# A sparse mixer on one core: keys in the partitions, softmax and gate as rows of the score product, row maxima and sums among the projections

## The reference, cut to what matters

```python
proj = x @ w_in                                   # q (16 heads x 64), 3 x (k, v) of 4 groups, 48 gates
q = q * HEAD_DIM ** -0.5
gates = sigmoid(gates)                            # one for each branch, head and query
k_cmp = gelu((blocks(k0) + pos0) @ w1_0 + b1_0) @ w2_0      # 31 blocks of 32 tokens, and v_cmp alike
s = q . k_cmp - slope * (t - center);  p_cmp = softmax(mask(s)) * m_c;  o_cmp = p_cmp @ v_cmp
s = q . k1 - slope * dist;  p = softmax(mask(s, dist >= 0));            o_sel = p @ v1
s = q . k2 - slope * dist;  p = softmax(mask(s, 0 <= dist < 512));      o_win = p @ v2
o = gates[0] * o_cmp + gates[1] * o_sel + gates[2] * o_win
return o @ w_out
```

## Time and profile before

| | |
|---|---|
| median of 3 runs | 3488.45 us (3485.4 to 3493.25) |
| profiled execution | 3480.47 us, span of its trace 3478.6 us |
| PE busy | 3188.6 us (92%) |
| VectorE busy | 1927.1 us (55%) |
| ScalarE busy | 1353.0 us (39%) |
| mean granted clock of PE | 0.951 |

### The profile page before, as it was taken

The page is one execution under the profiler, slowest core; times in us unless marked ns, Lnnn a source line. Parts: engine busy times, 40 slices in busy tenths (PEclk is TensorE's granted clock), DMA queues, the critical chain, the costliest instruction groups (busy, mean ns, idle before and its releaser), DMA issues.

```text
span 3478.6 us, 37759 instructions
## 1 busy us (share of the span) xinstructions
PE 3188.6 (92%) x15192; PEld 2546.7 (73%) x15192; DVE 1927.1 (55%) x2960; ACT 1353.0 (39%) x1980; POOL 192.1 (6%) x167
## 2 busy tenths in 40 slices
PE   6988899999999888899889888999999989899998
PEld 3876777777788666677667666888767879778876
DVE  5886666454433667754434774555245469455522
ACT  4244444334432344433443473333224336333321
POOL 0011122210000011100000000000000000000000
PEclk8999999999999899999989999999999879999999
DMA  6221123320012222232003122333322200123331
GB/s 213 71 67 55 57 66 94 99 89 26 23 37 73 73 69 77 58 93 81 25 25 91 55 77 80 97 91 97 92 76 97 79 1 1 49 88 94 91 97 61
DMA packets 77214, 250.93 MB, mean 72 GB/s; under 512 B 8689, under 2 KB 10609, under 8 KB 77041
## 3 DMA queue, kind: packets, MB, share of 16 engines
q1 hardware_dynamic: 71568, 228.60, 21.7%
q0 software_dynamic: 4608, 16.78, 1.6%
q10 hardware_dynamic: 864, 3.15, 0.2%
HBM read 246.39 MB, written 2.10 MB: 71 GB/s over the span
## 4 chain that ended last, share of the span: by engine, by line
PE 41%; DVE 7%; ACT 4%; issue 1%; DMA 0%; DVEq 0%; ACTq 0%; SPq 0%
PE PS L977 30%; PE PS L1410 2%; PE PS L2410 1%; PE PS L1533 1%; PE PS L996 1%; PE PS L2386 1%; ACT WH L938 1%; PE PS L2397 1%; DVE U L2194 1%; PE PS L2387 1%; DVE WL L948 1%; DVE U L1051 1%; PE PS L2333 0%; PE PS L2371 0%; DVE STAT L2664 0%
## 5 line engine op out<-in xcount | busy, mean ns | idle before, releaser
L948 DVE TENSOR_TENSOR WL<-RAW,WH 128x1024 fp32r<-128x1024 f32 (+3 forms) x415 | 485.7, 1171 | 587.4 <-ACT WH L938 586.4
L938 ACT ACTIVATE WH<-RAW 128x1024 fp32r<-128x1024 f32 (+4 forms) x447 | 429.2, 965 | 496.9 <-PE PS L977 399.3
L1410 PE MATMUL PS<-Hh,WH 128*128 128x512 f32 x1376 | 532.4, 387 | 16.7 <-DVE WL L948 8.1
L1410 PE MATMUL PS<-Hl,WH 128*128 128x512 f32 x1376 | 494.9, 360 | 0.0
L1410 PE MATMUL PS<-Hh,WL 128*128 128x512 f32 x1376 | 493.6, 359 | 0.0
L1410 PEld LDWEIGHTS PS<-Hh,WH 128*128 128x128 f32 x1376 | 266.8, 194 | 82.5 <-issue 25.0
L977 PE MATMUL PS<-FHh,WH 128*128 128x512 f32 x768 | 306.1, 399 | 15.1 <-DVE FHl L1042 14.9
L977 PE MATMUL PS<-FHl,WH 128*128 128x512 f32 x768 | 304.8, 397 | 0.0
L977 PE MATMUL PS<-FHh,WL 128*128 128x512 f32 x768 | 304.7, 397 | 0.0
L1410 PEld LDWEIGHTS PS<-Hl,WH 128*128 128x128 f32 x1376 | 266.4, 194 | 49.4 <-issue 11.3
L1410 PEld LDWEIGHTS PS<-Hh,WL 128*128 128x128 f32 x1376 | 265.3, 193 | 40.0
(11 more groups left out here) (347 smaller groups left out, 6003.6 us busy)
## 6 DMA issues: line engine op xcount, KB each, us to landing
RAW<-in_w_in SPq DMA_DIRECT2D x124, 512.0 KB, 3.6
RAW<-in_ffn_in SPq DMA_DIRECT2D x96, 512.0 KB, 3.6
RAW<-in_ffn_out SPq DMA_DIRECT2D x48, 512.0 KB, 3.5
MW<-in_w_ada SPq DMA_DIRECT2D x32, 384.0 KB, 4.1
RAW<-in_w_ada SPq DMA_DIRECT2D x32, 384.0 KB, 3.5
RAW<-in_nsa_in SPq DMA_DIRECT2D x21, 512.0 KB, 3.4
RAW<-in_lru_in SPq DMA_DIRECT2D x20, 512.0 KB, 3.6
BS<-in_bs POOLq DMA_DIRECT2D x16, 512.0 KB, 3.9
```

Source lines behind the costliest of these rows:

```text
L938: act.activation(WH[j % NSPL][:, 0:n], RAW[j % NRAW][:, 0:n], ACT.Copy).then_inc(*did("act_whi", ("whi", j)))
L948: dve.tensor_tensor(WL[j % NSPL][:, 0:n], RAW[j % NRAW][:, 0:n], WH[j % NSPL][:, 0:n].bitcast(F32), ALU.subtract).then_inc(*did("dve_wlo", ...
L1410: mm = pe.matmul(ps[:, c:c + w_], wt[:, 128 * k:128 * k + 128], x[:, a:a + w_], start=(k == 0 and q == 0), stop=(k == n - 1 and q == 2))
```

## The change

Nothing but the sparse mixer changes. Its work is cut into units, and one list of them (`norder`) sets the order on every engine.

- *Maxima and sums.* For each of 16 heads x 2 branches x 4 query tiles (128) a score product with queries in the partitions (`pe_nsa_max`) goes to one of two banks of its own. VectorE adds the bias from `TBH` (slope times distance, made once a head) and takes the row minimum of the negative into `NMX`, and ScalarE exponentiates in place and sums into `SUM`. These units are spread by `MOST`: 0.7 for each eighth of a linear from the sixth linear on, 0.35 in the last four, then 1.3 for each score step, until 128 are done. After every 32, `raise` takes the logarithm of the sums and forms, for each query and head, gate logarithm minus maximum minus log sum, split in two.
- *Rows.* Those values are transposed (`rows`) and put as four rows under the query rests in `Q2`; `NKL` gets ones in the matching rows, and more rows carry key position times slope. Rows 64 to 95 of the second score matmul so add bias, maximum, sum and gate.
- *Scores.* 80 steps (group, query tile, branch, key tile) have the keys in the partitions and four heads' queries as columns (`pe_nsa_scores`); tiles on the diagonal add a mask by a third matmul. ScalarE's exponential (no bias, no sum) gives probabilities that are already normalised and gated and already lie as the value product wants them. Values (`pe_nsa_values`) use 64 columns of the array for each half of the heads and add up in one bank over both branches; the compressed branch adds into the same bank (`cv`). Each query tile's result is split straight into `NQ` (`ev`).
- *Compression.* `CF` holds the plain slices, a fifth group holds the positions, whose product is added to the bias; the weights are taken in float32 from `RAW`, unsplit, and their copies `WH` and `WL` are numbered without them.
- The sigmoid of the gates becomes a log sigmoid by Exp and Ln. The compressed softmax keeps its form, its scores come as one matmul for both halves of the keys, and it stands among the last five linears. Its bias tables are loaded through GpSimd's queue. GpSimd copies the queries of groups 1 to 3 into `Q2`.

The core of the diff:

```diff
+MOST = (0.7, 0.35, 1.3)
...
+    def most(self, n):
+        for _ in range(n):
+            i = self.nmax
+            if i > 0:
+                self.unit("sum", i - 1)
+                if i % 32 == 0:
+                    self.unit("raise", i // 32 - 1)
+            if i == 128:
+                return
+            if i % 8 == 0:
+                self.unit("far", i // 8)
+            self.unit("max", i)
+            self.unit("least", i)
+            self.nmax += 1
...
+        turns = [0, 1, 12, 16, 2, 3, 8, 9, 20, 4, 10, 11, 5, 13, 17, 6, 7, 14, 15, 18, 19]
...
+                if i >= 5:
+                    share += MOST[0] if i < 17 else MOST[1]
+                    n = int(share)
+                    share -= n
+                    self.most(n)
...
+                g, j = parts[i][0], i % 20
+                self.unit("st", *parts[i])
+                if j == 0 and g < 3:
+                    self.unit("q2", g + 1)
+                share += MOST[2]
+                while share >= 1:
...
+                if j >= 12 and j % 2 == 0 and g < 3:
+                    self.unit("rows", g + 1, j // 2 - 6)
...
+            for q, (wt, x) in enumerate(((WH, NHh), (WH, NHl), (WL, NHh))):
+                mm = pe.matmul(ps[:, 0:S], wt[half[j]][:, 128 * k:128 * k + 128], x[:, k, :], start=(k == 0 and q == 0), stop=(k == 7 and q == 2))
...
+                j, acc = P.wj[u, 0], nbank.of(("acc", kv))
+                for k in range(8):
+                    at = 2 * (8 * c + k)
+                    x = CF[:, :, at:at + 512].rearrange("p g (j s) -> p g j s", s=16)[:, :, :, 0]
+                    for w in due("pe", ("raw", j), ("cf", kv, 0), ("cf", kv, 1), nbank.after["acc", kv]):
                         pe.wait_ge(*w)
+                    mm = pe.matmul(acc[:, 160 * m:160 * m + 160].rearrange("p (g j) -> p g j", g=5), RAW[j % NRAW][:, 128 * k:128 * k + 128], x, start=(c == 0 and k == 0), stop=(c == 1 and k == 7))
...
-                            for q, (wt, x) in enumerate(((WH, RH), (WH, RL), (WL, RH))):
-                                mm = pe.matmul(acc[:, 0:128], wt[j % NSPL][:, 128 * k:128 * k + 128], x[:, k, :], start=(c == 0 and k == 0 and q == 0), stop=(c == 1 and k == 7 and q == 2))
...
+        def pe_nsa_max(pe, u):
+            g, h, b, qt, c = nmax_of(u[1])
+            n, ps = 128 * qt + 128, mbank.of(u)
+            for w in due("pe", ("nq", h // 2), ("nk", b, g // 2), mbank.after[u]):
                 pe.wait_ge(*w)
+            pe.matmul(ps[:, 0:n], NQ[:, h, 128 * qt:128 * qt + 128], NKH[b][:, g, 0:n], start=True, stop=False)
+            pe.matmul(ps[:, 0:n], NQ[0:64, h, 128 * qt:128 * qt + 128], NKL[b][0:64, g, 0:n], start=False, stop=True).then_inc(*did("pe_max", u))
...
-                            mm = pe.transpose(ps[:, c:c + 128], pr[:, c:c + 128], ident)
...
+        def pe_nsa_scores(pe, u):
+            g, qt, b, kt = u[1:]
+            ps3 = P.sbank.of(u).rearrange("p (h q) -> p h q", h=4)
+            for w in due("pe", ("nrow", g, qt), ("q2", g) if g else ("q0", qt), ("q2c", g) if g else ("q0c", qt), ("k2", b), ("nk", b, g // 2), P.sbank.after[u]):
                 pe.wait_ge(*w)
+            pe.matmul(ps3, NKH[b][:, g, 128 * kt:128 * kt + 128], by_tile(NQ[:, 4 * g:4 * g + 4, :], qt), start=True, stop=False)
+            mm = pe.matmul(ps3, NKL[b][0:96, g, 128 * kt:128 * kt + 128], by_tile(Q2[g % 2][0:96, :, :], qt), start=False, stop=kt < qt)
+            if kt == qt:
+                for w in due("pe", ("masks", "n")):
+                    pe.wait_ge(*w)
+                mm = pe.matmul(ps3, IDN[:, :], MKN[:, :].unsqueeze(1).broadcast_to([128, 4, 128]), start=False, stop=True)
...
+        def pe_nsa_values(pe, u):
+            g, qt = u[1:3]
+            o = P.obank.of((g, qt))
+            if u[0] == "cv":
+                for w in due("pe", ("cpt", qt), ("cmp", 1)):
+                    pe.wait_ge(*w)
+                for i in range(4):
+                    f, m = i % 2, i // 2
+                    pe.matmul(o[64 * f:64 * f + 64, 128 * m:128 * m + 128], VB[:, g, 64 * i:64 * i + 64], PTC[qt][:, 128 * g:128 * g + 128], start=False, stop=False, skip_group_check=True)
+                return
+            b, kt = u[3:]
+            pt = PTN[P.pt.of(("st",) + u[1:])][:, :].rearrange("p (m f q) -> p f m q", m=2, f=2)
+            for w in due("pe", ("ex",) + u[1:], ("nv", b, g // 2), P.obank.after[g, qt]):
+                pe.wait_ge(*w)
+            for f in range(2):
+                mm = pe.matmul(o[64 * f:64 * f + 64, 0:256].rearrange("p (m q) -> p m q", m=2), VN[b][:, kt, g, :], pt[:, f, :, :], start=(b == 0 and kt == 0), stop=(b == 1 and kt == qt), skip_group_check=True)
...
-                                mm = pe.matmul(ps[:, o:o + 65], pt[:, c:c + 128], VN[b][:, k, g, :], start=(k == 0), stop=(k == nb - 1))
...
+                elif u[0] == "sum":
...
+                    for w in due("act", ("least", i)):
+                        act.wait_ge(*w)
+                    act.activation(ps, ps, ACT.Exp, bias=NMX[:, c:c + 1], scale=-1.0, accum_out=SUM[:, c:c + 1]).then_inc(*did("act_sum", u))
...
+                elif u[0] == "raise":
...
+                    act.activation(LSU[:, 32 * g:32 * g + 32], SUM[:, 32 * g:32 * g + 32], ACT.Ln).then_inc(*did("act_ln", ("lsu", g)))
...
+                elif u[0] == "rows":
...
+                    act.activation(by_tile(Q2[g % 2][64:68, :, :], qt), row_bank(u).of(u)[0:4, 0:512].rearrange("p (h q) -> p h q", h=4), ACT.Copy).then_inc(*did("act_row", ("nrow", g, qt)))
...
+                elif u[0] == "st":
+                    for w in due("act", u, [("pv",) + x[1:] for x in P.pt.after[u]]):
+                        act.wait_ge(*w)
+                    act.activation(PTN[P.pt.of(u)][:, :], P.sbank.of(u)[:, 0:512], ACT.Exp).then_inc(*did("act_ex", ("ex",) + u[1:]))
...
+                elif u[0] == "ev":
...
+                    act.activation(by_tile(NQ[:, 4 * g:4 * g + 2, :], qt), P.obank.of((g, qt))[:, 0:256].rearrange("p (m q) -> p m q", m=2), ACT.Copy).then_inc(*did("act_g", ("evh", g, qt)))
...
+                    dve.tensor_scalar(TBH[h % 2][:, :], TB[:, :], -SLOPES[h], None, ALU.mult).then_inc(*did("dve_far", u))
...
+                    dve.tensor_tensor_reduce(ps, TBH[h % 2][:, 512 - n:512], ps, -1.0, 3e38, ALU.add, ALU.min, NMX[:, c:c + 1]).then_inc(*did("dve_mx", u))
...
-                        dve.scalar_tensor_tensor(pj, tj, -SLOPES[s["h"] + j], pj, ALU.mult, ALU.add).then_inc(*did("dve_sb", ("sb", s["id"])))
...
+        def dve_raise(dve, g):
...
+            dve.tensor_tensor(RUP[:, at], NMX[:, at], LSU[:, at], ALU.subtract).then_inc(*did("dve_up", ("up0", g)))
...
+            dve.tensor_tensor(RUP[:, at], RUP[:, at], GLC[:, at], ALU.add).then_inc(*did("dve_up", ("up1", g)))
...
+            dve.tensor_copy(RUR[:, at], RUP[:, at]).then_inc(*did("dve_up", ("up2", g)))
+            two = RHL[:, 64 * g:64 * g + 64].rearrange("p (t h b z) -> p z t b h", t=4, h=4, b=2)
+            hi, full = (x[:, at].rearrange("p (t b h) -> p t b h", t=4, b=2) for x in (RUR, RUP))
...
+            dve.tensor_copy(two[:, 0, :, :, :], hi.bitcast(F32)).then_inc(*did("dve_up", ("up", g)))
+            dve.tensor_tensor(two[:, 1, :, :, :], full, hi.bitcast(F32), ALU.subtract).then_inc(*did("dve_up", ("up", g)))
```

More of the change, by code:

```diff
@@ L2783, in build, with pieces @@
             block.sync(sync_program)
+def pieces(v):
+    out = []
+    for _ in range(3):
+        m, e = math.frexp(v)
+        out.append(math.ldexp(round(m * 256) / 256, e))
+        v -= out[-1]
+    return np.array(out, np.float32)
 def constants():
```

1019 lines of the change are left out of this document (511 added, 508 removed).

## The result

| | before | changed |
|---|---|---|
| median of the runs | 3486.9 us (4 runs) | 3508.6 us (4 runs) |
| ratio, 95% interval | 1 | 1.0063 (1.0042 to 1.0084) |
| span of the profiled execution | 3478.6 us | 3504.1 us |
| first mixer linear to first output matmul | 396.1 us | 416.6 us (forecast 366) |

The change costs 0.6%. The forecast was 3458 and faster; 3508.6 lies 8.6 us above the upper end of the range. All medians in this document are of a kernel's undisturbed runs; three of the ten with value products in pairs took 3676 to 6113 us and are left out. The table by stretch of the changed kernel answers to the earlier trace rows: projections up to the first score matmul, the 36 score steps that carry maxima (the last maximum starts at 2939.78, the step behind it at 2941.10), the 44 that carry none.

What follows compares the result with a forecast made beforehand. TensorE was taken as the engine to count: projections 223, score steps 82 and 59, hand-over 2 make 366 us against 396.1, 30 less; from the runs' median of 3488.45 that gives 3458, range 3405 to 3500.

Steps and rivals of the forecast that it cites:

- the pause at 64 rows: Each maximum's second matmul on 64 array rows: 0.1 us in and 0.1 out; 25.6 us over all 128 maxima.
- the compression: Projections: 64 float32 matmuls of 160 columns at 0.27 us, 17.5 us in all, some 4 less than before.
- the score steps: 80 steps with keys in the partitions: 1.30 us of TensorE each, including 0.2 for two changes of partition.
- the clock: TensorE's products were priced at the upper clock throughout the stage, with 3.5 us added for the slow start.
- the slow start: First mixer linears: the second starts 9.1 us after the first, against 5.6; 3.5 us added.
- The waits: TensorE waiting: 18 us at dense linears, 8 among score steps, 4 for table loads, 5 at the projections' end.
- The second rival: Short waits all through the projections bring the lower clock: at 0.85, 25 us more, 3483; chance 0.12.
- the fourth rival: Value products' column halves run one after the other: 43 us more, 3501; chance 0.05.
- The third rival: The maxima's chain decides: 0.75 us of TensorE each, 66 us more, 3524; turns at 0.47 each; chance 0.13.
- The fifth rival: 46 of the 128 maxima stand among the scores, not the projections; already in the sum, no chance given.
- chance of 0.75 for faster: Whole kernel: 0.41 for the forecast, 0.28 for the first rival and half of the second rival's chance.
- The signs named at the end of the prediction: Trace readings for the mixer stage: 366 us in all, about 30 of waits, value pair spacing, 64-row pause, projections' clock.

## Why the prediction was wrong

Four terms of the sum were too low: the pause at 64 rows, the compression, the score steps, and the clock, which the sum put at nothing beyond the slow start. The waits were too high.

**The clock: the term that was left out.** The sum counts every product at the upper clock and adds 3.5 us for the slow start. Measured, the clock loss of the stage is 25 us, 19 of it among the projections at 0.92. The earlier trace rows had shown 0.95, 0.61 and 0.89 for the stretches before. The second rival named this (25 us more, at a clock of 0.85) with a chance of 0.12. Its size was near, though its sign, a clock under 0.9 in the projections, did not show: 0.92 was enough. +22 us. Which idle time makes the clock fall stays open.

**The compression: a price for the wrong form.** The 17.5 us stood on 0.27 a matmul "by columns", from float32 products over adjacent columns. For adjacent elements that is right (two records of 0.138). In the changed kernel a record took 0.27, and a matmul has two: 34.7 us, and the fp32 form costs 14 more than the 21 us of split products that it replaced, not 4 less. The diff showed the cause, an operand with one element of each 16, where the kernel before copied it together first. Sorting it gives back 18. +17 us.

**The pause at 64 rows: found, and mis-sized.** I took 0.1 in and 0.1 out from four transposes ahead of quarter tiles, called 0.2 the upper bound, and counted 25.6 us over 128 maxima. Measured inside a linear: 0.28 to 0.39, some 40 us over all by the estimate above; among the scores it came to about the 0.2 counted. The earlier trace rows showed only the way in. The way out (0.2) and the second product behind (0.1) could not be read there, and a single row of a "same sort of change" was no ground for an upper bound. With all rows the kernel is 34 us faster, of which some 13 are clock. So "doing it narrower" cost more than the arithmetic it saved. The rule of the Trainium skill ("TensorEngine Tiling (Array Packing)", Key Properties), that a change of tiling mode drains the array, agrees with the pauses at 64 rows (0.4 us at 512 columns) and column halves (0.38); 96 rows don't count as a change (0.337 against 0.338). +14 us.

**Score steps.** 1.30 us was the price, 0.2 of it for two changes; measured is 1.43, and the changes are 0.38. +10 us over 80 steps. The value pair at 0.45 (measured 0.42), side by side, was right, so the fourth rival falls; the earlier trace rows had it right.

**The waits.** 35 us were counted: 26 for the maxima's chain (18 and 8), 4 for table loads, 5 for the end of the projections. PE's idle time in the stage is 24.3, of which 19.9 is for sums. The mechanism and its place (L2445 waits for L2539) are right, the size near, and a third bank wins 32 with their cost in clock. The third rival's turning point, 0.47 us a maximum, was not reached: 19.9 / 128 is 0.16. But the pauses themselves hid part of the chain, as the waits of 30.8 without them show (0.24 a maximum), so a kernel without pauses would have been nearer to that rival than the prediction saw. The fifth rival, 46 maxima among the scores, is as counted. -11 us.

**The sum.** 366 + 22 + 17 + 14 + 10 less 11 is 418, and 416.6 was measured. The terms for clock and pauses are estimates, so that it closes this well is in part luck. The chance of 0.75 for faster (added up from 0.41, where the line above it has 0.42) rested on three prices that no row of before showed, all three taken from a neighbour and all three too low, and on a clock that the rows of before spoke against; the upper end of the range had no room for two of them at once.

The signs named at the end of the prediction: a value pair every 0.45, right; waits for sums about 30 us, 19.9; a pause of 0.1 behind a 64-row product, 0.2 and 0.1 more; 223 us up to the first score product, 255.5; a clock under 0.9 in the projections as a sign of being wrong, 0.92.

## What to carry to other kernels

A product over half of the array's rows among full ones was no saving here: price the way in, the way out and the product behind. For column halves the changes ate most of what running side by side gave (0.42 + 0.38 us a step, where one after the other would be some 0.9, an estimate from the 0.22 of the earlier trace rows). Putting several such products together helped where the engines behind had the buffers for it (value products) and cost 61 us where they did not (maxima). Work counted at the upper clock is a lower bound: look at the granted clock of the stretches before, since every kernel here lost between 6 and 41 us of this stage to it. Price each matmul with its operand's layout: a stride on the moving side doubled it here, and the copy ahead of it could sort at no cost that shows. Where results go from TensorE through two in-order queues, a third bank (32 us) was worth twice what shortening ScalarE's sums was (15).

## What the runs showed of the hardware

- A 64-row product between full ones of 512 columns: 0.1 us in, 0.2 out, 0.1 on the second product behind, 0.39 in all; 0.28 at 128 columns; 96 rows: nothing. Column halves: 0.10, 0.17, 0.11. At a change the weight load starts with its own product, elsewhere with the product ahead.
- A float32 record of 160 columns over a full array: 0.138 us with adjacent elements, 0.272 with elements 64 bytes apart.
- A sum along the row on ScalarE is an instruction more, 0.197 us, where VectorE's readout takes 0.140 (128 each):

```profile
L2539 ACT ACTIVATION_READ_ACCUMULATOR PS<-PS,NMX 128x1 f32 x128 | 25.3, 197 | 0.0
...
L2644 DVE DVE_READ_ACCUMULATOR2_ANT NMX<- 128x1 f32 x128 | 17.9, 140 | 0.1
```

- 15.4 us of short waits taken out of a stage of 417 gave 27.8: the rest came with the granted clock (0.92 to 0.98 over the projections, an estimated 25 us of loss to 6).
